# Two transformer blocks in fp32: more products of 512 columns, four filter taps on another engine, layer norm two units later

## The reference

```python
n = _rmsnorm(h, norm_mix_g[l])
z = n @ w_in[l]
c_a, c_g, q, k, v, qi, ki, wi, gc_logit, ga_logit = _split_cols(z, IN_SIZES)
...
g_conv = jax.nn.sigmoid(gc_logit + bg_conv)
g_attn = jax.nn.sigmoid(ga_logit + bg_attn)
y_conv = _conformer_conv(c_a, c_g, conv_w[l], conv_b[l], conv_ln_g[l], conv_ln_b[l], w_conv_out[l])
...
y_attn = _dsa_attention(qh, kh, vh, qih, ki, wih) @ w_attn_out[l]
h = h + (g_conv * y_conv + g_attn * y_attn) @ w_mix_out[l]
```

## Time and profile before

| what | value |
|---|---|
| time, median of 3 runs | 913.15 us (912.9 to 913.23) |
| profiled execution, its own time | 913.61 us |
| its span, first to last instruction | 911.7 us |
| PE busy | 904.4 us (99%), 5181 products |
| DVE busy | 678.7 us (74%) |
| ACT busy | 559.9 us (61%) |
| POOL busy | 40.7 us (4%) |
| mean granted TensorE clock | 0.999 of full |
| HBM read | 164.69 MB |

### The profile page before, as it was taken

How to read it: one execution, slowest core, us unless ns; L and a number is a source line. 1 busy time by engine, 2 the same in 40 slices (tenths; PEclk the granted TensorE clock), 3 DMA queues, 4 the chain that set the end, 5 groups by cost and what they waited for, 6 DMA issues and landing times.

```text
span 911.7 us, 13903 instructions
## 1 busy us (share of the span) xinstructions
PE 904.4 (99%) x5181; PEld 783.1 (86%) x5181; DVE 678.7 (74%) x1181; ACT 559.9 (61%) x993; POOL 40.7 (4%) x48
## 2 busy tenths in 40 slices
PE   9999999999999999999999999999999999999997
PEld 7899987788888888888999998888789888888886
DVE  5879976367776666667699999997786776666666
ACT  6746768755655544546667778865945764554454
POOL 0300000000000000000011212100000000000000
PEclk9999999999999999999999999999999999999999
DMA  9954544465556556555589999976475356555551
GB/s 332 319 169 140 162 140 148 176 232 184 184 159 200 200 186 210 194 197 161 187 213 274 254 262 280 238 223 197 139 240 174 116 163 225 189 185 185 185 185 47
DMA packets 93698, 179.03 MB, mean 196 GB/s; under 512 B 7808, under 2 KB 12736, under 8 KB 93376
## 3 DMA queue, kind: packets, MB, share of 16 engines
q1 hardware_dynamic: 88800, 165.30, 55.6%
q0 software_dynamic: 4464, 12.32, 7.4%
q10 hardware_dynamic: 368, 0.52, 0.2%
HBM read 164.69 MB, written 1.05 MB: 182 GB/s over the span
## 4 chain that ended last, share of the span: by engine, by line
PE 99%; DVE 0%; issue 0%; DVEq 0%; ACT 0%; ACTq 0%
PE pb L444 96%; PE pb L448 3%; DVE X L2347 0%; DVE MSQ L2385 0%; DVE XS L2394 0%; ACT ST L1566 0%; DVEq L55 0%; DVE DG L2140 0%; PE pb L829 0%; DVE ST L2369 0%; DVE ST L2364 0%; DVEq L2346 0%; ACTq L1565 0%
## 5 line engine op out<-in xcount | busy, mean ns | idle before, releaser
L1613 DVE TENSOR_TENSOR wlo<-raw,whi 128x1024 fp32r<-128x1024 f32 (+1 forms) x298 | 353.5, 1212 | 109.1 <-ACT whi L1031 108.7
L1031 ACT ACTIVATE whi<-raw 128x1024 fp32r<-128x1024 f32 (+1 forms) x304 | 309.6, 1039 | 137.0 <-PE pb L444 114.5
L444 PE MATMUL pb<-XT,whi 128*128 128x256 f32 (+2 forms) x1456 | 312.2, 330 | 0.7 <-issue 0.7
L444 PEld LDWEIGHTS pb<-XT,whi 128*128 128x128 f32 (+1 forms) x1456 | 239.8, 190 | 20.3 <-issue 2.1
L444 PE MATMUL pb<-whi,ZO 128*128 128x512 f32 (+1 forms) x808 | 251.8, 389 | 0.0
L444 PE MATMUL pb<-XT,wlo 128*128 128x256 f32 (+1 forms) x1032 | 209.2, 282 | 0.0
L444 PEld LDWEIGHTS pb<-whi,ZO 128*128 128x128 f32 x808 | 151.3, 188 | 31.6 <-DVE wlo L1613 1.0
L444 PEld LDWEIGHTS pb<-XT,wlo 128*128 128x128 f32 (+1 forms) x1032 | 168.0, 190 | 8.7
L444 PE MATMUL pb<-whi,XT 128*128 128x512 f32 (+1 forms) x544 | 170.9, 390 | 0.0
L444 PE MATMUL pb<-wlo,ZO 128*128 128x512 f32 (+1 forms) x404 | 156.6, 388 | 0.0
L444 PEld LDWEIGHTS pb<-whi,XT 128*128 128x128 f32 x544 | 101.6, 188 | 21.3 <-issue 0.9
(11 more groups left out here) (251 smaller groups left out, 629.5 us busy)
## 6 DMA issues: line engine op xcount, KB each, us to landing
raw<-in_w_in SPq DMA_DIRECT2D x105, 512.0 KB, 5.0
raw<-in_w_ff SPq DMA_DIRECT2D x64, 512.0 KB, 5.1
raw<-in_w_up SPq DMA_DIRECT2D x32, 512.0 KB, 4.7
raw<-in_w_down SPq DMA_DIRECT2D x32, 512.0 KB, 5.6
YC<-PRODS POOLq DMA_DIRECT2D x16, 384.0 KB, 6.5
PRODS<-PRODS POOLq DMA_DIRECT2D x14, 384.0 KB, 7.7
raw<-in_w_branch_b SPq DMA_DIRECT2D x8, 512.0 KB, 5.1
raw<-in_w_out SPq DMA_DIRECT2D x8, 512.0 KB, 3.9
```

What stands on the lines that cost most here:

```text
L444: return e.matmul(o, l, r, start=start, stop=stop, skip_group_check=True)
L1031: return e.activation(o, i, ACT.Copy, scale=scale)
L1613: e.tensor_tensor(wlo[u % NW][:, 0:c], raw[u % NRAW][:, 0:c], whi[u % NW][:, 0:c].bitcast(F32), ALU.subtract).then_inc(lo, 1)
```

## The change

Four parts. (1) b2_qi, b2_k0 and b2_k1, 12 units, are made by `cols_pair` and joined by `copy_left` on ACT and `add_right` on DVE. (2) The first taps of channel tiles 4 to 7 go from DVE to ACT, where they stand between `run("b2_ca1")` and `run("b2_qi")`. (3) TAPS is cut anew for the 151 taps that are left: none at the last unit's place of b2_k0 and b2_k1, and the last ones at the first unit of b2_ga1. (4) `conv_norm` begins two units later on all three engines.

```diff
-TAPS = (0,) + (4,) * 6 + (0,) + (4,) * 3 + (6, 6) + (4,) * 5 + (4, 3) * 3 + (3,) + (1,) * 9 + (3,) * 18
+TAPS = (0,) + (4,) * 6 + (0, 5, 5, 4, 1, 6) + (4,) * 5 + (4, 3, 0, 3, 4, 3, 0) + (1,) * 9 + (3,) * 20
-HALVES = ("b1_c0", "b2_cg0", "b2_ca0")
+HALVES = ("b1_c0", "b2_cg0", "b2_ca0", "b2_qi", "b2_k0", "b2_k1")
...
@@ PE, attention2: waits for the joined queries and keys
+                            e.wait_ge(*out_at["b2_qi", 3])
...
+                        e.wait_ge(*out_at[f"b2_k{h // 4}", h % 4])
                         e.wait_ge(*out_at[f"b2_q{h // 4}", h % 4])
...
@@ PE, conv_norm
-                yield
+                for _ in range(3):
+                    yield
                 e.wait_ge(ln_tiles, 1)
                 mm(PB[7][:, 0:256], ones, LNS[0], True, True).then_inc(ln_sum, 1)
...
@@ PE, order of the groups
-            for name in ("b2_cg1", "b2_ca1", "b2_qi"):
-                cols(name, XT, ready)
+            cols("b2_cg1", XT, ready)
+            cols("b2_ca1", XT, ready)
+            cols_pair("b2_qi", XT, ready)
...
             for name in ("b2_k0", "b2_k1", "b2_q0", "b2_q1"):
-                cols(name, XT, ready, side)
+                (cols_pair if name in HALVES else cols)(name, XT, ready, side)
...
@@ ACT, conv_norm
-                yield
-                yield
+                for _ in range(4):
+                    yield
                 e.wait_ge(ln_sum, 1)
...
@@ ACT, order of the groups
             run("b2_ca1", products)
+            for f in range(4, 8):
+                e.wait_ge(*out_at["b2_ca1", f - 4])
+                e.activation(YC[:, f, :], U2[:, f, 0:256], ACT.Identity, bias=prm("convb2", f),
+                             scale=prm("convw2", f)).then_inc(first_taps, 1)
             run("b2_qi", products)
-            copy_cols("b2_qi", QI)
+            for f in range(4):
+                copy_left("b2_qi", f, QI[:, f, :])
...
@@ DVE, taps
-                    for k in range(31):
+                    for k in range(int(fs != (3,)), 31):
...
-                                e.wait_ge(*(out_at["b2_ca1", f - 4] if f >= 4 else (halves_in, f + 1)))
+                                e.wait_ge(halves_in, f + 1)
...
-                                e.wait_ge(dve_step, made[c])
+                                e.wait_ge(*((dve_step, made[c]) if c in made else (first_taps, f - 3)))
...
@@ DVE, conv_norm and order of the groups
+                yield
+                yield
                 e.wait_ge(y_made, 5)
...
             run("b2_qi", taps)
+            for f in range(4):
+                add_right("b2_qi", f, QI[:, f, :])
             run("b2_ki", taps)
...
                 run(name, side, taps)
+                for f in range(4) if name in HALVES else ():
+                    add_right(name, f, KT2[:, 4 * int(name[4]) + f, :])
...
+            norm = conv_norm()
+            run("b2_ga1", side, taps, norm)
             now(taps)
-            norm = conv_norm()
-            run("b2_ga1", side, norm)
```

More of the change, by code:

```diff
@@ L268, in build @@
         out_a, out_d = sem("tile_out_act"), sem("tile_out_dve")
-        by_act = {"b1_q", "b1_kv", "b1_w", "b1_c1", "b1_gb0", "b1_gb1", "b1_ga0", "b1_ga1", "mv", "mk", "b2_cg1", "b2_qi", "b2_ki", "b2_k0", "b2_k1", "b2_q0", "b2_q1", "b2_v0", "b2_v1"}
+        by_act = {"b1_q", "b1_kv", "b1_w", "b1_c1", "b1_gb0", "b1_gb1", "b1_ga0", "b1_ga1", "mv", "mk", "b2_cg1", "b2_ki", "b2_q0", "b2_q1", "b2_v0", "b2_v1"}
         tile_at, out_at, bank_of, bank_free = {}, {}, {}, {}
@@ L343, in build @@
         y_made, mk_joined = sem("y_made"), sem("cross_keys_joined")
+        first_taps = sem("first_taps_made")
         prod_made, prod_joined = sem("tap_products_made"), sem("odd_taps_joined")
@@ L1496, in scalar_program @@
                 run(name, side, products)
-                copy_cols(name, KT2 if name[3] == "k" else QT2, 4 * int(name[4]))
+                if name[3] == "k":
+                    for f in range(4):
+                        copy_left(name, f, KT2[:, 4 * int(name[4]) + f, :])
+                else:
+                    copy_cols(name, QT2, 4 * int(name[4]))
             for name in ("b2_v0", "b2_v1", "b2_gc0", "b2_gc1"):
```

## The result

The changed kernel takes 918.97 us (median of 6 runs, 917.69 to 919.76) against 913.18 us for the kernel before (median of 6, 912.47 to 913.89). The ratio is 1.0062, with a 95% interval of 1.0051 to 1.0072: slower by 0.6%. The forecast was 917.3, with 914.4 to 919.3 as the range.

What follows compares the result with a forecast made beforehand. PE was taken as the bound, with DVE full beside it from 470 to 484 us. Terms −1.08 + 2.4 + 0.6 + 2.2 = +4.1 on the median of 913.15 gave 917.3 us; range 914.4 to 919.3, about 0.8 likely.

Steps and rivals of the forecast that it cites:

- the three places: New PE waits were forecast at the banks of b2_qi, at those of b2_k1, and at z_lo.
- Longer products: In the 12 pair units on PE, 0.09 us saved a unit, −1.08 us in all.
- Queries: Ahead of b2_ki, PE waits for DVE's first addition, late behind ACT's first taps and copy: +2.4 us.
- Keys: Ahead of b2_q0, PE waits for DVE's addition after b2_k1: +0.6 us, ends 0 and 0.8; nothing after b2_k0.
- Layer norm: At z_lo around b2_wc0, PE waits 1.1, 0.3 and 1.4 us, less 0.6 won back: +2.2 us.
- 0.57: In b2_wc0, time the kernel before lost to late high parts, which the change would win back: −0.6 us.
- (a): The forecast itself: all three places wait, about 917.3 us, ends 915.5 to 919, chance 0.72.
- a hold of 0 to 1.2: On DVE, gate adds and a low part delay the layer norm's mean subtraction by 0 to 1.2 us; 0.9 taken.
- (b): Only one of the two large waits, at b2_ki or in the layer norm, comes: 915.1 or 914.5 us, chance 0.14.
- the first case: b2_ki finds its bank free, so the queries lose their 2.4 us wait: 915.1 us.
- Rival (d): TensorE's clock falls at a stop, one unit at half clock costing 2.8 us: 920.1 us, chance 0.06.

Runs made afterwards that it cites:

- recut: Changed kernel with the owed high part before ACT's first taps, the layer norm's old start, and fewer taps ahead of the joins; 912.19 us, ratio 0.9986.
- gates_early: As recut, but ACT makes the four gate sigmoids ahead of the layer norm's root; 911.97 us, ratio 0.9985.
- norm_alone: The kernel before, with only the layer norm's start moved two units later on PE, ACT and DVE; 916.00 us, ratio 1.0030.
- norm_back: The changed kernel with only the layer norm's move undone; 916.71 us, ratio 1.0039.
- taps_dve: As recut, but the four first taps stay on DVE, 155 taps in all; 914.71 us, ratio 1.0015.
- norm_one_hi: As hi_first, but the layer norm starts one unit later than in the kernel before, not two; 917.71 us, ratio 1.0048.
- after_again: The changed kernel run again unchanged; 919.17 us, ratio 1.0063 to the kernel before.
- long_stop: The changed kernel with an unread extra copy on ACT ahead of each of the four first taps; 921.85 us, ratio 1.0095.
- hi_first: The changed kernel, but ACT makes the owed high part before the four first taps, not behind them; 915.96 us, ratio 1.0032.
- both_back: The changed kernel with the owed high part before ACT's first taps and the layer norm's old start; 913.63 us, ratio 1.0003.
- gate_behind_hi: As hi_first, but DVE makes the gate product of b2_wa1 behind all z_lo; 916.66 us, ratio 1.0036.
- qi_plain: The changed kernel with b2_qi made by plain products and copied out by ACT, as before; 915.69 us, ratio 1.0026.

## Why the prediction was right, and where its sum was off

Direction, range and the three places were right; the forecast was 1.7 us short: 1.0 in the sum at full clock, the rest by the clock. Point by point:

**Longer products, −1.08.** b2_k0 shows it undisturbed: 13.22 to 12.87, 0.0875 a unit. recut saves 0.28 in b2_qi, 0.35 and 0.27 in the keys, 0.06 in mk: −0.95. The rule of the Trainium skill ("TensorE: Matmul & The Clock Gate", section "Wait — 56ns, not 53.3ns?"), by which 12 units would save an estimated 0.24 us, is not borne out here.

**Queries, +2.4.** DVE's rows came as added up: from the low part to the first addition 483.98 − 473.49 = 10.49, and 10.44 was the sum. b2_qi costs 13.88 − 11.18 = 2.70 over the same group without a stop.

**Keys, +0.6.** 11.96 − 11.25 = 0.71, and none at b2_k0, as said.

**Layer norm, +2.2.** The variance was late as taken (it begins at 642.66, 1.16 behind the end of b2_wa1's first unit at 641.50), and by the way that was taken: DVE's low part ahead of it waits for ACT's copy behind the four sigmoids. The first z_lo begins 650.85 − 642.66 = 8.19 behind it (8.57 to its end was the sum). Three stops come to 3.0: ga1 to wc0 take 48.36, and 45.36 in gates_early, which has none. What before lost there was not 0.57 but 45.74 − 45.36 = 0.38. In all +2.62.

So at full clock −0.95 + 2.70 + 0.71 + 3.0 − 0.38 = +5.1, where I had +4.1. No single term did it; the stops were priced too low by 0.6 in all (2.70 for 2.4, 0.71 for 0.6, 3.0 for 2.8: the way from an engine's end to PE's next product, 0.14 us at b2_ki and 0.10 at b2_q0, was left out, and may be part of it), the 0.57 too high by 0.2 and the saving by 0.13.

**Luck in the range.** The ends named for (a), keys 0 to 0.8 and a hold of 0 to 1.2 (the variance 0.7 earlier, when PE's sum is there, or 0.3 later), give 916.0 to 917.8, not 915.5 to 919; nothing in the working gives the 919. The runs at full clock (918.3 in the median) lie above 917.8, and all but one of the late ones (919.7 in the median) above the range's 919.3. The median of 918.97 is the mean of the slowest early run (918.36) and the fastest late one (919.58): with one more late run in place of an early one it would have been over 919.3, outside, for any late time measured. In (b) the price of the first case is 914.9 by the sum's own terms, not 915.1. That the profiled run of the change stood at 917.69, just where the text had put it (917.7), is chance: its first 20 units took a microsecond less than in the profile of before.

**The clock.** Rival (d) was priced at one unit at half the clock, 2.8 us, with a chance of 0.06. It is real: in 6 of 11 runs of the change (five at a mean clock of 0.997 and one at 0.998 that is counted by its time), at 1.5 us in the profile that has it. Those runs lie at 919.7 (median), the others at 918.3. The chance was far too low; that no window of before shows such a fall said nothing, since no stop of that length was in it. The rule of the Trainium skill, same page, section "What's actually happening", that an idle engine goes back to the lower level, agrees with the 0.50 in two profiles.

**The change's parts by themselves.** The layer norm's move costs 2.6 (norm_alone, norm_back). Its cause is order: the gate's products and sigmoids have a fixed place, and the norm was moved past them (one unit later is worse than two, 4.5 by the groups). The first taps on ACT are worth their place only behind the owed copy: there they cost nothing and save 1.5 us of waiting in b2_ga1 (taps_dve). The pairs save 0.95 once fewer taps stand ahead of the joins.

What stays open: why a stop of 2.5 us brings the clock down in some runs and not in others, how much of the stops' 0.6 is the way from engine to engine, and the last 1.0 us of taps_dve.

## What to carry to other kernels

When work moves into another engine's program, look at what stands behind its wait there, not at the engine's busy share: ACT was 61% busy, and four activations of 0.5 us and a wait in front of one copy cost 2.2 us, which an exchange of the two gave back. When a bank or buffer is let go by a busier engine than before, the releasing instruction needs its own slot in that engine's order; here two to four taps less ahead of it made the difference between −0.95 and nothing. And a stop of the matrix engine can have two prices: its length, and products behind it at half the clock (in some runs with the 2.5 us of this change, in all four with 3.7). The second price shows as two groups of times before it shows in a profile.

## What the runs showed of the hardware

- With a stop of 2.5 us on PE, 6 of 11 runs of the change and 3 of 5 of norm_back came late or with a mean clock of 0.996 to 0.997, and one of four of norm_one_hi showed 0.997; with one of 3.7 us 4 of 4 did. The two profiles taken of such runs (after_again, long_stop) show the granted clock at 0.50 behind the stop. Kernels whose longest stop after the start was at most 1.3 us showed no mean clock under 0.998 (hi_first, both_back, recut, norm_alone, gate_behind_hi, qi_plain, taps_dve, gates_early).
- The clock can fall after PE has begun again: in after_again PE's products have full spacing from 486.20 to 486.99, then the double, and full again from 490.19, while PE is busy throughout. In long_stop it fell inside the stop already (mean 0.80 in 484 to 486 us, PE idle). The price differed with it: 1.5 us and 2.4 us.
- ACT loads the table for an activation ahead of the wait of its instruction, so in the changed order it costs nothing: the load at 645.45 is over at 646.73, and the activation waits for DVE until 649.77. The one at 641.51 ends at 642.79, and its activation waits for DVE until 643.11.

```profile
645.45 1.28 ACT L1372 ACT_TABLE_LOAD   x1
649.77 0.60 ACT L1372 ACTIVATE YC<-YC,PR 128x256 f32<-128x256 f32 x1 [3.04 <-DVE YC L2124]
```
